# Layer 0 of a transformer block: projection, mLSTM heads, differential attention and output projection as one stage of jobs and tiles

## The reference, cut to what matters

```python
def even_layer(x, c, ctx, c_ctx, ...):
    u, uc = modulate(x, ...), modulate(ctx, ...)
    p = u @ w_in
    q_m, k_m = silu(conv3(p[mq])), silu(conv3(p[mk]))        # 8 heads of 64
    v_m, o_m = p[mv], p[mo]
    ig_f, lf_f, ig_b, lf_b = mlstm_gates(p[mg])
    # the same of the context tokens: k, v and gates
    h_m = mlstm_mixer(...)      # forward and backward scan from the context's state
    # h = rmsnorm(h_f + h_b) * sigmoid(o)
    h_d = diff_mixer(...)       # 4 heads, q and k in two halves of 64, axial rope
    # p = softmax(s1) - lam * softmax(s2) over 512 keys; rmsnorm(p @ v) * (1 - lam_init)
    mix = concatenate([h_m, h_d]) @ w_out
    x = x + gt_m * rmsnorm(mix, mix_post_g)
```

## Time and profile before

| | us |
|---|---|
| median of 3 runs | 2280.55 (2279.08 to 2283.31) |
| the profiled execution | 2284.5 |
| its span | 2282.7 |
| PE busy in the span | 2055.9 |

### The profile page before, as it was taken

The page is one execution under the profiler, slowest core; times in us unless marked ns, Lnnn a source line. Parts: engine busy times, 40 slices in busy tenths (PEclk is TensorE's granted clock), DMA queues, the critical chain, the costliest instruction groups (busy, mean ns, idle before and its releaser), DMA issues. The chain is left out here.

```text
span 2282.7 us, 54026 instructions
## 1 busy us (share of the span) xinstructions
PE 2055.9 (90%) x23610; PEld 1792.8 (79%) x23610; DVE 865.7 (38%) x2350; ACT 390.5 (17%) x1152; POOL 14.5 (1%) x21
## 2 busy tenths in 40 slices
PE   6999966899978766999999999999986999879986
PEld 4668835788867655999999999999985877668765
DVE  3672552577766822010111101011113375234762
ACT  2211441100014122000001000000001133121331
POOL 0000000000000000000000000000000000000000
PEclk7999977999989986999999999999997899888998
DMA  9544002599962121989899898989881232222200
GB/s 390 203 166 185 19 1 74 203 348 335 359 247 95 54 74 39 372 317 372 331 365 346 327 374 317 381 329 366 329 329 56 82 159 75 92 94 117 86 1 19
DMA packets 66943, 480.86 MB, mean 211 GB/s; under 512 B 7312, under 2 KB 8592, under 8 KB 8720
## 3 DMA queue, kind: packets, MB, share of 16 engines
q1 hardware_dynamic: 66704, 477.35, 55.3%
HBM read 476.27 MB, written 1.05 MB: 209 GB/s over the span
## 5 line engine op out<-in xcount | busy, mean ns | idle before, releaser
L1461 PE MATMUL PS<-sb_arena,sb_ring 128*64 128x98 f32 x11264 | 485.8, 247 | 5.2 <-issue 4.4
L1461 PEld LDWEIGHTS PS<-sb_arena,sb_ring 128*64 128x64 f32 x11264 | 478.4, 136 | 14.9 <-issue 11.0
L461 PE MATMUL PS<-sb_U,sb_ring 128*128 128x256 f32 (+1 forms) x1456 | 387.8, 426 | 40.6 <-PEq L208 40.6
L461 PEld LDWEIGHTS PS<-sb_U,sb_ring 128*128 128x128 f32 x1456 | 291.3, 203 | 121.7 <-issue 81.5
L1477 PE MATMUL PS<-sb_arena,sb_ring 128*64 128x98 f32 x5632 | 250.4, 248 | 1.4 <-issue 1.4
L1477 PEld LDWEIGHTS PS<-sb_arena,sb_ring 128*64 128x64 f32 x5632 | 240.0, 137 | 14.2 <-ACT sb_arena L1617 10.9
L1650 DVE TENSOR_TENSOR sb_arena<-PS,sb_arena 128x98 f32<-128x98 f32 x176 | 45.7, 260 | 448.8 <-ACT sb_arena L1592 448.8
L611 PE MATMUL PS<-sb_U,sb_ring 128*128 128x256 f32 x704 | 159.2, 385 | 7.7 <-PEq L208 7.7
L611 PEld LDWEIGHTS PS<-sb_U,sb_ring 128*128 128x128 f32 x704 | 133.9, 193 | 25.9 <-issue 8.1
L385 DVE SCALAR_TENSOR_TENSOR sb_arena<-sb_ring,sb_cs,sb_arena 128x256 f32<-128x256 f32 x280 | 135.8, 485 | 10.0
L461 PE MATMUL PS<-sb_arena 128*64 128x128 f32 (+6 forms) x724 | 120.1, 346 | 14.5 <-DVE sb_arena L1307 11.3
(11 more groups left out here) (288 smaller groups left out, 1719.2 us busy)
## 6 DMA issues: line engine op xcount, KB each, us to landing
sb_ring<-stream SPq DMA_DIRECT2D x450, 1024.0 KB, 5.9
sb_consts<-consts SPq DMA_DIRECT2D x1, 1729.0 KB, 26.5
sb_U<-ctxT SPq DMA_DIRECT2D x1, 1024.0 KB, 7.0
sb_XT<-xT SPq DMA_DIRECT2D x1, 1024.0 KB, 8.8
out<-sb_XT SPq DMA_DIRECT2D x1, 1024.0 KB, 3.8
sb_small<-small SPq DMA_DIRECT2D x1, 292.0 KB, 2.8
sb_consts<-consts SPq DMA_DIRECT2D x1, 129.0 KB, 2.7
sb_all_small<-layer_small SPq DMA_DIRECT2D x1, 110.0 KB, 26.6
```

Of the source, the lines that this page charges most:

```text
L461: ins = pe.transpose(o, l, r) if t.turn else pe.matmul(o, l, r, start=s, stop=e)
L1461: ins = pe.matmul(PS[c:c + 64, m % 4, h * T:h * T + n], w[:, h, kt, c:c + 64], src[:, kt, 0:n], start=(kt == 0), stop=(kt == KT - 1))
```

## The change

The stages `in0`, `mlstm`, `mnorm`, `mturn`, `diff`, `dnorm`, `dturn` and `out0` become one `project` named `layer0`, with a list of tasks:

- gates, then mq and mk tiles in turn with two gate steps after each, the four mv0 tiles, the turned gates;
- for h = 0 to 7: `decays(h)`, a tile, `head_out(h-1)`, `scores(h)`, in later heads more tiles. The tiles are in `M_BESIDE`;
- dq1, dk1, a rope, `head_out(7)`, the head norm as a chain of six tasks;
- for i = 0 to 9: `differ(i-1)` (the difference of the two softmaxes), `branch_scores(i)`, tiles of `D_BESIDE`, `turn_probs0(i-1)`, tiles, `values0(i-2)`; at i = 7 also the turns of the mLSTM part, the first half of the output projection (`oa0` to `oa7`, at i = 7 to 9) and the norm of three of the four heads;
- the norm of the last head, and the second half of the output projection, added to the first on DVE.

`project` gets a `tail` of chunks that have no side chunks between them, and `Task` gets `after` (tasks that the emptying engine waits for) and `peek` (a task that reads a bank that another empties). The weights of `w_in` and `w_out` are reordered in the stream to match. Sigmoid becomes Tanh with scale and bias, the norm gains go into the gate and into the scale of a copy, and the two normed factors of the softmax difference become one: exp1 - (lam sum1/sum2) exp2, scaled by 1/sum1 at the end. `attention` and the other stage builders are deleted.

```diff
+IN0_UNITS = ("gates", "", "mq0", "mk0", "mq1", "mk1", "mq2", "mk2", "mq3", "mk3", "mv0", "", "mv1", "", "dq0", "dk0", "dv0", "",
+             "dq1", "dk1", "om0", "om1", "dq2", "dk2", "dv1", "", "dq3", "dk3", "om2", "om3")
...
-        def project(name, n, tasks, side=None):
+        def project(name, n, tasks, side=None, tail=0):
...
+            main = main + [n + n_side + k for k in range(tail)]
+            n += tail
...
+                            for other in t.after:
+                                wait_done(eng, other)
+                            if t.matmuls or t.peek:
+                                fill = (t if t.matmuls else t.peek).fill
+                                eng.wait_ge(bank_full, fill)
...
+        for m in range(4):
+            for name, x, rhs, segs, col in ((f"mq{m}", qm[:, m, :], UX, [(0, 0)], m), (f"mk{m}", km[:, m, :], U2, [(0, 0), (C, C)], 4 + m)):
+                conv = tile(name, rhs, "dve", conv3(x, col, segs))
+                silu = add(None, None, "act", lambda act, b, link, x=x: nc.scalar.activation(x, x, ACT.Silu), (conv,))
+                spread(2)
...
+                out.append(add(None, matmuls, "act", f, (gates_done, silu), after=(turned_gates,) + ((n_done[h - 2],) if h >= 2 else ())))
...
+            s_done[h] = [add(None, matmuls_of(s0), "dve", f_of(s0), after=tuple(decayed)) for s0 in (0, 2)]
...
+            n_done[h] = add(None, matmuls, "dve", f, tuple(s_done[h]) + tuple(v_ready[h // 4]), serial=True)
...
+                fills.append(add(None, lambda bank, chunk, b=b: [(bank, dq[halves[b], h, t * P:(t + 1) * P], dk[halves[b], h, :], True, True)],
+                                 "act", f, tuple(d_ready) + tuple(n_done[x] for x in (6, 7)), after=((done["turned", i - 3],) if i >= 3 else ())))
...
+        M_BESIDE = (("mv10",), ("mv11",), ("mv12",), ("mv13",), ("dq0",), ("dk0", "rope"), ("dv00", "rope", "dv01"), ("dv02", "dv03"))
+        D_BESIDE = (("dq1", "dk1", "rope"), ("rope", "om0", "om1"), ("dq2", "dk2", "rope"), ("rope", "dv10", "dv11"), ("dv12", "dv13"),
+                    ("dq3", "dk3", "rope", "rope"), ("om2", "om3"), ("oa0", "oa1", "oa2"), ("oa3", "oa4", "oa5"), ("oa6", "oa7"))
+        for h in range(NH):
+            decayed = decays(h)
+            beside(*M_BESIDE[h][:1])
+            if h:
+                head_out(h - 1)
+            scores(h, decayed)
+            beside(*M_BESIDE[h][1:])
+        beside(*D_BESIDE[0])
+        head_out(NH - 1)
+        h_normed = norm_chain(Hm.rearrange("p t h d -> p (t h) d"), 16, 64, sq0, st0, n_done[NH - 1])
+        for i in range(len(jobs) + 2):
+            if 0 <= i - 1 < len(jobs):
+                differ(i - 1)
+            if i < len(jobs):
+                branch_scores(i)
+            if i == 7:
+                for m in range(4):
+                    turn_mixed(m, lambda t, m=m: Hm[:, t, 2 * m:2 * m + 2, :].rearrange("p h d -> p (h d)"), h_normed)
+            if i:
+                beside(*D_BESIDE[i][:1])
+            if 0 <= i - 1 < len(jobs):
+                turn_probs0(i - 1)
+            if i:
+                beside(*D_BESIDE[i][1:])
+            if 0 <= i - 2 < len(jobs):
+                values0(i - 2)
+            if i == 7:
+                diff_norm(slice(0, 3), done["out", 5])
+        diff_norm(slice(3, 4), done["out", 7])
+        for m in range(KT):
+            chunk, matmuls = out_tile(m, 1)
+            add(chunk, matmuls, "dve", lambda dve, bank, link, m=m: dve.tensor_tensor(big[:, m, :], bank[:, 0:T], big[:, m, :], ALU.add),
+                tuple(o_turned[k] for k in range(4, 8)), after=(first_half[m],))
```

More of the change, by code:

```diff
@@ L1035, in build, with spread @@
         gate_step("act", lambda e: nc.scalar.activation(gN[0:8, :, 1, :], B8[:, :, C:], ACT.Exp, scale=-1.0))
+        gates_done = gate_steps[-1]
+        def spread(n):
+            for _ in range(n):
+                if gate_steps:
+                    tasks.append(gate_steps.pop(0))
         def turn_gates(bank, chunk):
@@ L1063, in build @@
-        tasks += waiting
-        def silu_of(x, need):
-            return Task(None, None, "act", lambda act, b, link: nc.scalar.activation(x, x, ACT.Silu), (need,))
-        for m in range(8):
+        for m in range(4):
[3 more added lines that the diff above has]
+                spread(2)
@@ new lines, in build, with rope_one, sigmoid_tile, f @@
+        ax = ("rot_ax", "cos_ax", "sin_ax")
+        raw, d_ready, o_ready = [], [], []
+        def rope_one():
+            x, need = raw.pop(0)
+            tasks.append(rope_task(x, x, rtmp0, *ax, need))
+            return tasks[-1]
+        def sigmoid_tile(m):
+            def f(act, bank, link):
+                link(nc.scalar.activation(om[:, m, :], bank[:, 0:T], ACT.Tanh, scale=0.5))
+                return nc.scalar.activation(om[:, m, :], om[:, m, :], ACT.Identity, scale=hg[:, m:m + 1], bias=hg[:, m:m + 1])
+            t = tile(f"om{m}", UX, "act", f)
+            t.after = (consts_done,)
+            return t
@@ L1068, in build, with turn_mixed, matmuls @@
+        o_turned = {}
+        def turn_mixed(m, src, need):
+            def matmuls(bank, chunk):
+                return [(bank[:, t * P:(t + 1) * P], src(t), ident, True, True) for t in range(2)]
             if m < 4:
-                tasks.append(tile_task(5 + m // 2, m % 2, UX, "dve", conv3(qm[:, m, :], m, [(0, 0)])))
-            else:
-                tasks.append(tile_task(5 + m // 2, m % 2, U2, "dve", conv3(km[:, m - 4, :], m, [(0, 0), (C, C)])))
-            waiting = waiting[8:] + [silu_of(qm[:, m, :] if m < 4 else km[:, m - 4, :], tasks[-1])]
@@ new lines, in turn_probs0 @@
+        def turn_probs0(i):
+            done["turned", i] = add(None, lambda bank, chunk: [(bank[:, s * P:(s + 1) * P], PB[i % 3][:, 0, s * P:(s + 1) * P], ident, True, True)
+                                                               for s in range(4)], "act",
+                                    lambda act, bank, link: nc.scalar.activation(PT[:, i % 2, :], bank, ACT.Copy),
+                                    (done["differ", i],), turn=True, after=((done["out", i - 2],) if i >= 2 else ()))
@@ new lines, in values0, with f @@
+        def values0(i):
+            h, t = jobs[i]
+            S_ = ST[:, i % 3, :]
+            def f(act, bank, link):
+                link(nc.scalar.activation(Hd[:, t, h, :], bank[:, 0:P], ACT.Copy, scale=S_[:, 12:13]))
+                return nc.scalar.activation(sq1, Hd[:, t, h, :], ACT.Square, accum_out=ss[:, t, h:h + 1])
+            done["out", i] = add(None, lambda bank, chunk: [(bank[:, 0:P], PT[:, i % 2, s * P:(s + 1) * P], dv[:, s, h * P:(h + 1) * P],
+                                                             s == 0, s == 3) for s in range(4)], "act", f, (done["turned", i],))
@@ new lines, in out_tile, with matmuls, out_first @@
+        def out_tile(m, half):
+            def matmuls(bank, chunk):
+                w = chunk.rearrange("p (n k c) -> p n k c", n=4, k=4)
+                return [(bank[:, 0:T], w[:, m % 4, k, :], mixT[:, 4 * half + k, :], k == 0, k == 3) for k in range(4)]
+            return IN0_CH + 2 * half + m // 4, matmuls
+        first_half = []
+        def out_first(m):
+            chunk, matmuls = out_tile(m, 0)
+            first_half.append(add(chunk, matmuls, "act", copy_to(big[:, m, :]), tuple(o_turned[k] for k in range(4))))
```

563 lines of the change are left out of this document (214 added, 349 removed).

## The result

| | median, us | range, us | ratio to the kernel before, 95% |
|---|---|---|---|
| before (6 runs) | 2281.57 | 2272.68 to 2283.31 | |
| changed (6 runs) | 2266.5 | 2262.09 to 2271.53 | 0.9937 (0.9919 to 0.9954) |
| predicted | 2268.5 | 2256 to 2280 | |

What follows compares the result with a forecast made beforehand. PE was taken as the bound. In layer 0's 332.1 us, 293.3 of full-clock work plus 16.6 idle, 8.0 slow clock and 2.5 waits gave 320.4, 11.7 won: 2268.5 us forecast, range 2256 to 2280.

Steps and rivals of the forecast that it cites:

- work at full clock: Layer 0 stretch: PE's 303.6 us busy time less 10.3 us of slow clock, 293.3 us.
- idle: PE idle left by the new order, from the last mLSTM head to the output tiles: 16.6 us.
- slow clock: PE running slower behind the five idles: 8.0 us in all, with ends 0 and 15.
- waits: 226 waits of 16 scores tasks in PE's queue: 2.5 us taken, between 0 and 13.
- 8.1, 1.1, 1.9, 3.1, 2.4: PE idles in us: into the attention, before scores(6), before oa0, first difference norm's turns, end before second-half output tiles.
- The 8.1: Into the attention: 2.0 us before scores(0), then 6.1 us before the first transposes, while DVE does norm, maximum and difference.
- The rival of a slow clock through the whole job loop: First stall to last output tile: stalls keep the clock down, 0.75 granted costs 31 us, result 2291; chance 0.07.
- nearer the low row, for a full tile stands in front of most: Scores tasks: why 2.5 us was taken for waits, between 0 and 13 us.
- pile of waits: Rival at the scores tasks: waits cost 8 to 13 us or paired scores lose overlap, 2275 to 2281; chance 0.13.
- The first stretch, the heads, the weights: Projection with gates, mLSTM heads, and weight stream: each was to add no time and win none, 0 us.
- Carrying over to the end: Stages behind the changed part run as before, so the 11.7 us won there reaches the kernel's end.
- The cost of a table change: First difference norm on ACT: load taken at 1283 ns; at the skill page's 2.66 us, 1.4 us more, result 2270.

Runs made afterwards that it cites:

- all_edits_2: Changed kernel with one wait per engine, tiles, turns and rotary steps moved at attention start and tail, first difference norm later; 2239.8 us, 0.9807 of the kernel before.
- again: The changed kernel run once more with no edit; 2266.55 us, ratio 0.9934 to the kernel before.
- waits_layer0: Changed kernel with only the latest need of each engine waited for on PE, in this stage alone; 2257.93 us, 0.9890 of the kernel before.
- bare_all: Changed kernel with no tiles between mLSTM heads or attention jobs, output tiles after the last norm; 2271.77 us, 0.9957 of the kernel before.

## Why the prediction was right, and where it was lucky

`all_edits_2` gives what the prediction had to work out: the work at full clock is at most 289.3 us, its busy time. With it the changed kernel's stage of 316.5 us (`again`) splits into terms. Idle is 16.3. Its busy time is 10.9 above 289.3; that of `waits_layer0`, the same order without the surplus waits, is 6.2 above, so 6.2 is slow clock and 4.7 the waits, each good to some 2 us. By the clock records of the two traces PE was busy at the low level for 23.4 us of the stage in `again` and for 19.9 in `waits_layer0`; half of such time is lost, so up to 1.7 of the 4.7 may be slow clock. (The first profile of the changed kernel had 2.3 us more of busy time.)

| term | predicted | measured |
|---|---|---|
| work at full clock | 293.3 | at most 289.3 |
| idle | 16.6 | 16.3 |
| slow clock | 8.0 | 6.2 |
| waits | 2.5 | 4.7 |
| stage | 320.4 | 316.5 |

**Work at full clock: 4.0 too high.** I took the slow clock out of the stretches behind 285.1 and left what lay ahead of it: by the granted clocks of the earlier trace rows some 6 us (16.8 x 0.17 + 159.9 x 0.01 + 60.9 x 0.03), of which `all_edits_2` still has some. For instance, of two equal tile groups in the projection of the kernel before the second ran slow, 1.7 us:

```profile
159.80 14.06 PE L461 MATMUL PS<-sb_ring,sb_U 128*128 128x256 f32 x64
...
191.60 15.77 PE L461 MATMUL PS<-sb_ring,sb_U 128*128 128x256 f32 x64
```

**Idle: right, place by place but one.** Predicted 8.1, 1.1, 1.9, 3.1, 2.4; measured 5.6, 1.6, 2.3, 3.1, 2.8, and 0.9 ahead of scores(3). The 8.1 is right in its chain and wrong in its split. DVE's queue was as walked through:

```profile
234.92 1.22 DVE L1062 TENSOR_REDUCE sb_rstd<-sb_arena 128x16 f32<-128x1024 f32 x1 [1.12 <-ACT sb_arena L1061]
...
236.92 1.23 DVE L1066 TENSOR_TENSOR sb_YT<-sb_YT,sb_rstd 128x1024 f32<-128x1024 f32 x1
238.18 1.42 DVE L1100 TENSOR_REDUCE sb_mean<-PS 128x1 f32<-128x512 f32 x2
...
241.87 0.75 DVE L1119 SCALAR_TENSOR_TENSOR sb_arena<-sb_arena,sb_mean 128x512 f32<-128x512 f32 x1
```

Head norm, then the row maximum, then the difference: the first transposes start 11.0 us after the last head, where 8.1 + 2.6 = 10.7 had been worked out. But the scores and the rotary step between the two stalls took 5.5 us instead of 2.6, at half clock (granted clock 0.56 from 231.6 to 242.6), so 2.9 us stand as busy what I had as idle. Job 3's 0.9 comes from the same place in the code as job 6's: scores(3) names the rotary step of dq2, which it doesn't use.

**Slow clock: the right size.** 6.2 for 8.0. Behind the last head PE was busy at the low level for 13.0 us in `again` and 19.3 in the first profile, half of which is 6.5 and 9.7. The rival of a slow clock through the whole job loop is excluded: the granted clock is 0.97 from 242.6 to 316.9, and over the stretch that the prediction meant, from the last head to the end, it is 0.91, as it had been taken.

**Waits: mis-sized.** The step that failed is "nearer the low row, for a full tile stands in front of most". In layer 2 a task has four waits and no gap was seen; here 10 to 19 stand in a pile. All 226 at 0.058 us would be 13 us, and what the surplus costs is 4.7 to 5.4 us by the stage and 7.3 to 8.6 by the medians: the tile in front hides between a third and two thirds of it, where I had taken four fifths (2.5). The rival "pile of waits" had the price and the loss of the side-by-side scores right, and the medians reach its low end; the stage doesn't. The forecast held because work at full clock erred by 4.0 the other way: that is luck.

**The first stretch, the heads, the weights: 0, as said.** No gap in 165.3 us.

**What the prediction left out.** It counted the joining of stages as idle time that "is gone if cover is found". `bare_all` shows two thirds of the gain, 9.8 of 15 us, without a tile between jobs; some 5 of these are the cover of the last head, and the rest came with the fences (6.6 us less idle ahead of the attention). How much joining wins with nothing covered was not run. The sum came out right because it was made from the idle times left over and not from the tiles that were moved.

**Carrying over to the end.** 13.2 us arrive at the norm behind the stage (its matmuls start at 380.35 before and 367.13 after); the median moved by 15.1. Between profiles all that follows differs by up to 7 us (1898 to 1905), most of it in PE's idle time there (174.5 to 180.5 us).

The cost of a table change, weighed in the prediction, is settled for this kernel by these rows of the changed kernel (ACT, first difference norm):

```profile
329.44 0.19 ACT L1135 ACTIVATION_READ_ACCUMULATOR sb_arena<-sb_arena 128x1 f32 x1
329.65 1.28 ACT L1143 ACT_TABLE_LOAD   x1
...
330.94 0.21 ACT L1143 ACTIVATE sb_rstd<-sb_rstd 128x6 f32<-128x6 f32 x1
```

The load begins 0.02 us after the operation ahead and the next follows 0.01 us behind it: 1.3 us in all. The Trainium skill, page "ScalarE: Activation LUTs", section "What ACT_TABLE_LOAD costs", has 2.66 with a drain; no such wait is seen here, and the measurement decides.

## What to carry to other kernels

Find the order by walking each engine's queue and summing the idle time that is left, and then look at what each remaining wait names: a need that the task doesn't use (two of the stalls here were for rotary steps of a later head), a chain that stands in a queue ahead of something urgent, a transpose placed right behind the chain that feeds it. Moving a handful of such items and dropping the surplus waits won 26.7 us here, more than the change itself. Joining stages pays by itself too, since a fence makes serial what could overlap: 6.6 us of idle at the one place measured. Waits that another wait implies should be left out, above all ahead of short matmuls meant to run side by side.

## What the runs showed of the hardware

Waits on PE's queue cost time although nothing was left to wait for: 0.058 us each when 210 that repeat earlier ones were added, and they part two matmuls that would otherwise run side by side (2.90 us for 2.11).

An idle time doesn't by itself set the clock behind it. The first difference norm's turns waited 3.09 us in the changed kernel and 3.09 in `waits_layer0`. Behind them (stretches, columns as above, clock third from the end):

```profile
331.80:336.00 4.20, 4.11 (x14) 3.52 (x15) 3.95 (x11) 1.33 (x3) 0.00 (x0) 0.59 0.00 0
```

```profile
324.90:327.80 2.90, 2.81 (x16) 2.33 (x17) 2.73 (x9) 1.20 (x3) 0.00 (x0) 1.00 0.00 0
```

The same six transposes and eight records of output matmuls ran mostly at the 1.2 GHz level in one and at 2.4 GHz in the other. The changed kernel had stood still for 2.30 us and run partly at the low level some 10 us earlier (320.36 and 323.45 above), `waits_layer0` had stood still nearly as long (2.16) and its next tiles ran at full clock. Why the one fell isn't settled here; in `all_edits_2`, where no idle behind the last head reaches 0.8 us, the clock didn't fall there.
